# Attention projection by seven products: GpSimd's work given to VectorE, the rotation limited to 1024 tokens, block sums made in the out projection

## The reference

```python
hs = rms_norm(xs, norm_g[i]) * (1.0 + sc_s) + sh_s          # 1024 latent tokens; hp the same for 128 context tokens
q, k, v, g = jnp.split(h @ w_in, 4, axis=-1)                # w_in is 1024 x 8192, 8 heads of 256 in each of q, k, v, g
qs, ks_ = apply_rope(qs, cos, sin), apply_rope(ks_, cos, sin)   # x * cos + rot * sin, latent tokens only
out = gated_out(rms_norm(attend(q, k, v)) * c, g, w_out)    # (o * silu(g)) @ w_out
x = x + gate * out
```

## Time and profile before

| | |
|---|---|
| median of three runs | 2240.91 us |
| the profiled execution's own time | 2238.06 us |
| its span on the core | 2236.2 us |
| TensorE busy | 2135.9 us (96%) |
| VectorE busy | 1356.4 us (61%) |
| ScalarE busy | 888.6 us (40%) |
| GpSimd busy | 105.1 us (5%) |
| mean granted clock of TensorE | 0.985 |

### The profile page before, as it was taken

The page is one execution under the profiler, slowest core; times in us unless marked ns, Lnnn a source line. Parts: engine busy times, 40 slices in busy tenths (PEclk is TensorE's granted clock), DMA queues, the critical chain, the costliest instruction groups (busy, mean ns, idle before and its releaser), DMA issues. The chain is left out here.

```text
span 2236.2 us, 33058 instructions
## 1 busy us (share of the span) xinstructions
PE 2135.9 (96%) x13347; PEld 2035.8 (91%) x13347; DVE 1356.4 (61%) x2034; ACT 888.6 (40%) x1648; POOL 105.1 (5%) x44
## 2 busy tenths in 40 slices
PE   8999999989997999999999999999999999999997
PEld 3999877989997999999999999999999999989997
DVE  4777464763257877878755332228888888875223
ACT  4511142232123333333334243336666666665110
POOL 0000000000003222222200000000000000000000
PEclk9999999999998999999999999999999999999999
DMA  8455342784233444455545534443444433307332
GB/s 331 137 175 181 122 151 100 256 311 146 81 120 119 133 138 149 134 139 148 157 144 184 207 135 161 164 159 142 161 160 160 160 137 114 124 1 264 114 127 85
DMA packets 124824, 342.70 MB, mean 153 GB/s; under 512 B 14337, under 2 KB 69761, under 8 KB 114433
## 3 DMA queue, kind: packets, MB, share of 16 engines
q1 hardware_dynamic: 124672, 340.61, 44.5%
HBM read 225.70 MB, written 114.82 MB: 152 GB/s over the span
## 5 line engine op out<-in xcount | busy, mean ns | idle before, releaser
L2032 PE MATMUL o_ps<-o_y_hi,o_w 128*128 128x384 f32 x1536 | 395.0, 337 | 14.8 <-DVE o_y_lo L2141 13.3
L2032 PEld LDWEIGHTS o_ps<-o_y_hi,o_w 128*128 128x128 f32 x1536 | 280.3, 190 | 16.3 <-DVE o_y_lo L2141 13.7
L2032 PE MATMUL o_ps<-o_y_lo,o_w 128*128 128x384 f32 x768 | 258.4, 336 | 0.0
L2433 ACT ACTIVATE a_e<-a_ps,a_nmax 128x1152 f32<-128x1152 f32 x127 | 155.3, 1223 | 62.8 <-DVE a_nmax L2494 62.8
L2390 PE MATMUL a_ps<-a_v_hi,a_at_hi 128*128 128x256 f32 x576 | 173.0, 300 | 0.0
L2494 DVE TENSOR_REDUCE a_nmax<-a_ps 128x1 f32<-128x1152 f32 x127 | 171.8, 1353 | 0.2 <-PE a_ps L2357 0.2
L2390 PE MATMUL a_ps<-a_v_lo,a_at_hi 128*128 128x256 f32 x576 | 162.4, 282 | 0.0
L2390 PE MATMUL a_ps<-a_v_hi,a_at_lo 128*128 128x256 f32 x576 | 162.2, 282 | 0.0
L2032 PEld LDWEIGHTS o_ps<-o_y_lo,o_w 128*128 128x128 f32 x768 | 145.7, 190 | 0.0
L915 PE MATMUL p_ps<-p_late_hi,p_w_hi 128*128 128x384 f32 x384 | 128.9, 336 | 2.4 <-DVE p_late_lo L1202 2.3
L2141 DVE TENSOR_TENSOR o_y_lo<-o_y_raw,o_y_hi 128x384 fp32r<-128x384 f32 x96 | 51.9, 555 | 128.6 <-ACT o_y_hi L2086 128.4
(11 more groups left out here) (321 smaller groups left out, 5435.3 us busy)
## 6 DMA issues: line engine op xcount, KB each, us to landing
p_w_raw<-w_in_dram SPq DMA_DIRECT2D x32, 1024.0 KB, 6.9
o_y_raw<-y_dram SPq DMA_DIRECT2D x96, 192.0 KB, 3.6
g_wada<-w_ada_dram SPq DMA_DIRECT2D x16, 1024.0 KB, 6.8
f_w_raw<-w_u_dram SPq DMA_DIRECT2D x32, 512.0 KB, 4.3
o_w_raw<-w_out_dram SPq DMA_DIRECT2D x32, 512.0 KB, 4.3
g_dram<-g_stage SPq DMA_DIRECT2D x16, 576.0 KB, 3.2
f_g<-g_dram SPq DMA_DIRECT2D x8, 1152.0 KB, 7.6
y_dram<-f_y SPq DMA_DIRECT2D x8, 1152.0 KB, 5.3
```

Source lines behind the costliest of these rows:

```text
L2032: mm = pe.matmul(ps[:, d, 0:CH], a, m, start=(e == 0 and j == 0), stop=(e == ET - 1 and j == 2))
L2433: act.activation(split3(e[:, m % 2, half, :]), ps[:, 3 * half:3 * half + 3, 0:CH], ACT.Exp, bias=nmax[:, m % 2, half:half + 1], scale=1.0, ...
```

## The change

- GpSimd has no instruction left in `project`.
- The four input block sums are made by VectorE at the end of the out projection of layer 0 (`mix`, at tile 5), in place in the normed x (`block`) instead of in tiles of their own. To make room, the norm of the first 768 tokens moves from tile 4 to tile 2 and its high and low halves from tile 5 to tile 4.
- In `project`, VectorE makes the weight block sums of unit 1 and cuts t2 before it norms the late tokens; ACT cuts t2 and t0 before it copies the norm's factors. The order of the further cuts is new, and the eviction of unit 0 (`unload`) waits until the sums in whose place it writes are cut.
- The rotation's two additions are VectorE's, directly behind "third", and cover the 1024 latent tokens alone, as does the sine product. turned_lo(0) and turned_lo(1) move to before "far_near" and "near_far", ahead of the weight block sums. The block sums are in the order 0, 1, 2, 3, and the first pair's high half waits for two of them.
- In `values`, the weights for the next head are cut ahead of the fifth step (at == 4) and not ahead of the first.

```diff
+    def block(self, k, c):
+
+        return self.x[:, 4 * k:4 * k + 4, c * CH:(c + 1) * CH]
...
-        t_sum = [at(f"t{k}_sum", [P, DT // 2, CH], 24576 + 6144 * k) for k in range(4)]
+        t_sum = [tiles.block(k, c) for k, c in ((0, 0), (1, 1), (0, 1), (1, 0))]
...
                 if n == 1:
-                    pe.wait_ge(t_lo_done, 1)
+                    pe.wait_ge(t_lo_done, 3)
                 else:
                     pe.wait_ge(combined, summed(n - 1, "second"))
                 product(Z2, sums_of(1), mixed(1), True, True).then_inc(proj_done, 1)
                 pe.wait_ge(snapped, 2 * (n - 1) + 1)
                 product(Z1, weights(0, 1), quarter(1, 0), False, True).then_inc(proj_done, 1)
                 pe.wait_ge(s_lo_done, s_ready(n, 1))
-                if n == 1:
-                    pe.wait_ge(t_lo_done, 2)
-                else:
+                if n > 1:
                     pe.wait_ge(combined, summed(n - 1, "far_near"))
                 product(Z4, sums_of(2), mixed(2), True, True).then_inc(proj_done, 1)
-                if n == 1:
-                    pe.wait_ge(t_lo_done, 3)
-                else:
+                if n > 1:
                     pe.wait_ge(combined, summed(n - 1, "near_far"))
                 product(Z3, sums_of(0), mixed(0), True, True).then_inc(proj_done, 1)
...
-            for b in range(2):
+            act.wait_ge(t_summed, 4)
+            inverse_rms.root(act)
+            mixed_hi(2)
+            mixed_hi(0)
+            inverse_rms.copies(act)
+            for d in range(DT):
+                act.wait_ge(t_done, 2 * DT + d + 1)
+                for tok, which in PIECES:
+                    op = act.activation(tiles.late_hi[:, d, tok], tiles.x_late[:, d, tok], ACT.Identity,
+                                        bias=sh.mod[:, LAYER, d, which:which + 1])
+                op.then_inc(h_hi_done, 1)
+
+            def unload(b):
                 act.wait_ge(proj_done, made(0, f"late{b}"))
+                act.wait_ge(t_lo_done, 2)
                 act.copy(made_x[0][:, b, 0:2 * CH].rearrange("p (c t) -> p c t", c=2),
                          ps[:, WHOLE[b][0]:WHOLE[b][1] + 1:WHOLE[b][1] - WHOLE[b][0], 0:CH]).then_inc(evicted, 1)
                 act.copy(made_x[0][:, b, chunk(2)], ps[:, LATE[b], 0:CH]).then_inc(evicted, 1)
+
+            sums_hi(1, 0)
+            mixed_hi(1)
+            sums_hi(1, 1)
+            act.wait_ge(proj_done, made(0, "late0"))
+            tiles.split_hi(act, 1, 0)
+            unload(0)
+            mixed_hi(3)
+            unload(1)
...
-                if n >= 2:
+                if n == 1:
+                    act.wait_ge(t_lo_done, 4)
...
-                    turned_hi(n - 1, 0)
-                    if n + 1 < UNITS:
-                        sums_hi(n + 1, 0)
-                    turned_hi(n - 1, 1)
-                else:
-                    if n - ROPE in (2, 4):
-                        past_split((n - ROPE) // 2 - 1)
-                    if n + 1 < UNITS:
-                        sums_hi(n + 1, 0)
+                    for b in range(2):
+                        turned_hi(n - 1, b)
+                elif n - ROPE in (2, 4):
+                    past_split((n - ROPE) // 2 - 1)
+                if n + 1 < UNITS:
+                    sums_hi(n + 1, 0)
...
-                if j + 1 < H:
+                def next_hi():
...
                 for at, t in enumerate(ORDER):
+                    if at == 4 and j + 1 < H:
+                        next_hi()
...
+            def sums(n):
+
+                dve.wait_ge(raw_in[n % 2], 16 * (n // 2) + 16)
+                if n > 1:
+                    dve.wait_ge(proj_done, made(n - 1, "near_far"))
+                    dve.wait_ge(s_lo_done, s_ready(n - 1, 1))
+                dve.tensor_tensor(s_sum[:, 0], block_of(n, 1, 0), block_of(n, 1, 1), ALU.add).then_inc(s_summed, 1)
+                dve.wait_ge(s_summed, 4 * (n - 1) + 1)
+                dve.tensor_tensor(s_sum[:, 1], s_sum[:, 0], block_of(n, 0, 0), ALU.subtract).then_inc(s_summed, 1)
+                dve.tensor_tensor(s_sum[:, 2], block_of(n, 0, 0), block_of(n, 1, 0), ALU.subtract).then_inc(s_summed, 1)
+                dve.wait_ge(s_summed, 4 * (n - 1) + 2)
+                dve.tensor_tensor(s_sum[:, 3], block_of(n, 0, 1), s_sum[:, 1], ALU.subtract).then_inc(s_summed, 1)
...
-                    dve.wait_ge(t_summed, 4)
+                    dve.wait_ge(t_lo_done, 4)
...
-                dve.scalar_tensor_tensor(turned[:], made_x[n % 2][:], SCALE if n < H else 1.0,
-                                         cs[:, 1:2, :].to_broadcast([P, 2, T]), ALU.mult, ALU.mult).then_inc(sined, 1)
+                dve.scalar_tensor_tensor(turned[:, :, 0:NS], made_x[n % 2][:, :, 0:NS], SCALE if n < H else 1.0,
+                                         cs[:, 1:2, 0:NS].to_broadcast([P, 2, NS]), ALU.mult, ALU.mult).then_inc(sined, 1)
...
+            def rotate(n):
+                dve.wait_ge(cosined, n + 1)
+                for b in range(2):
+                    x = made_x[n % 2][:, b, 0:NS]
+                    dve.tensor_tensor(x, x, turned[:, 1 - b, 0:NS], ALU.add if b else ALU.subtract).then_inc(rotated, 1)
...
-            sums(1, (2, 0, 1, 3))
-            for k, m in enumerate((1, 2)):
-                mixed_lo(m, k + 1)
+            sums(1)
+            dve.wait_ge(shift_done, 1)
+            mixed_lo(2, 1)
+            for d in range(DT + 1):
+                if d < DT:
+                    norm(d)
+                if d > 0:
+                    low_half(d - 1)
+            mixed_lo(0, 2)
             sums_lo(1, 0)
-            mixed_lo(0, 3)
+            mixed_lo(1, 3)
+            tiles.split_lo(dve, 1, 0, w_ready(1, 0))
             sums_lo(1, 1)
             mixed_lo(3, 4)
-            tiles.split_lo(dve, 1, 0, w_ready(1, 0))
...
+                if n <= ROPE:
+                    rotate(n - 1)
                 dve.wait_ge(combined, summed(n, "third"))
                 dve.wait_ge(snapped, 2 * (n - 1) + 2)
                 dve.tensor_tensor(far(n)[:, chunk(1)], far(n)[:, chunk(1)], far(n)[:, chunk(0)], ALU.add).then_inc(combined, 1)
+                if n <= ROPE:
+                    turned_lo(n - 1, 0)
                 dve.wait_ge(combined, summed(n, "far_far"))
                 add(n, "far_near", far(n)[:, chunk(0)], Z4, near(n)[:, chunk(1)], "far_near")
-                dve.wait_ge(combined, summed(n, "far_near"))
-                add(n, "near_far", near(n)[:, chunk(1)], Z3, near(n)[:, chunk(1)], "near_far")
-                if n + 1 < UNITS:
-                    sums(n + 1, (2, 0, 1, 3))
-                if n <= ROPE:
-                    turned_lo(n - 1, 0)
-                if n + 1 < UNITS:
-                    sums_lo(n + 1, 0)
                 if n <= ROPE:
                     turned_lo(n - 1, 1)
                 elif n - ROPE in (2, 4):
                     past_split((n - ROPE) // 2 - 1)
+                dve.wait_ge(combined, summed(n, "far_near"))
+                add(n, "near_far", near(n)[:, chunk(1)], Z3, near(n)[:, chunk(1)], "near_far")
+                if n + 1 < UNITS:
+                    sums(n + 1)
+                    sums_lo(n + 1, 0)
...
-                if j + 1 < H:
+                def next_lo():
...
                 for at, t in enumerate(ORDER):
+                    if at == 4 and j + 1 < H:
+                        next_lo()
...
-        @block.gpsimd
-        def _(pool):
-            for semaphore in x_stored:
-                pool.wait_ge(semaphore, 16 * NCH)
-            pool.wait_ge(t_done, 2 * DT)
-
-            def x_of(k, c):
-                return tiles.x[:, 4 * k:4 * k + 4, c * CH:(c + 1) * CH]
-
-            pool.tensor_tensor(t_sum[0][:], x_of(0, 1), x_of(0, 0), ALU.subtract).then_inc(t_summed, 1)
-            pool.wait_ge(t_summed, 1)
-            pool.tensor_tensor(t_sum[1][:], x_of(1, 1), t_sum[0][:], ALU.subtract).then_inc(t_summed, 1)
-            pool.wait_ge(t_summed, 2)
-            pool.tensor_tensor(t_sum[2][:], x_of(1, 1), x_of(0, 1), ALU.subtract).then_inc(t_summed, 1)
-            pool.tensor_tensor(t_sum[3][:], x_of(1, 0), t_sum[1][:], ALU.subtract).then_inc(t_summed, 1)
-
-            def rotate(n, b):
-                pool.wait_ge(cosined, n + 1)
-                x = made_x[n % 2][:, b, :]
-                pool.tensor_tensor(x, x, turned[:, 1 - b, :], ALU.add if b else ALU.subtract).then_inc(rotated, 1)
-
-            for n in range(ROPE):
-                for b in range(2):
-                    rotate(n, b)
...
-                if following is not None and d == 5:
+                if following is not None and d == 4:
...
+            def mix(block):
+
+                near, far = [block(k, 0) for k in range(2)], [block(k, 1) for k in range(2)]
+                dve.wait_ge(following.h_lo_done, LAST * DT)
+                dve.tensor_tensor(near[0], far[0], near[0], ALU.subtract).then_inc(following.t_summed, 1)
+                dve.wait_ge(following.t_summed, 1)
```

(14 more changed lines are left out.)

52 lines of the change are left out of this document (10 added, 42 removed).

## The result

The changed kernel took 2187.79 us (median of 4 runs, 2185.70 to 2189.32), beside 2241.93 of the kernel before on the same chip (4 runs): a ratio of 0.9756 with an interval of 0.9738 to 0.9774. 2190.5 had been predicted, range 2184 to 2202. The medians differ by 54.1 where 50.4 was forecast; of the 3.7 between, 1.0 went to the kernel before, which took 2241.93 here and not 2240.91. The profiled execution took 2189.32, its span is 2187.5.

The account below looks back on a forecast made before the run. TensorE was taken as busy nearly everywhere, so only its idle or low-clock stretches could give time: 10.3 + 2.8 + 26.9 + 10.4 = 50.4 us off 2238.06, plus 2.85 to the median, gives 2190.5, range 2184 to 2202.

Parts of the forecast that it names:

- The start of the stage and unit 1: Project stage: late norm without GpSimd's sums beside it, 11.2 us less up to unit 1; unit 1 itself 2.8 less.
- rival 4: The clock falls in the 1.6 us gap before unit 1 and the tail costs 3.5: 2196 us, 3 in 100.
- The tail: End of the out projection: norm moved earlier and block sums added on VectorE delay tile 7's eviction, 0.9 us lost.
- The value stage: Head 0: weight conversion behind the fourth eviction removes TensorE's wait and the lower clock behind it, 10.4 us saved.
- Rival 2: The value stage keeps its wait, the gate's store landing over 2.7 us later: 2200 us, 6 in 100.
- Units 2 to 16: Rotation units of the attention projection: pitch falls from 24.79 to 23.0 us, 26.9 us saved over 15 units.
- The ring: Rotation units: sine waits for the previous unit's low-half stores, cut after block sums, setting the pitch (24.0 and 25.7 us).
- Rivals 1 and 5: Low-half stores still late (2198 or 2205 us, 12 in 100); ring lengthens (2249, 1 in 100) or VectorE bounds (2231, 1).

Follow-up runs that it names:

- Experiment 5: Kernel before, with GpSimd's four input block sums made by VectorE at the project stage's start, ahead of the late norm: 2232.84 us against 2239.46 (0.9974).
- experiment 4: Kernel before, with only the value stage's move, the next head's weights cut behind the fourth eviction: 2230.46 us (0.9951).
- Experiment 1: Kernel before, with VectorE's low halves and ScalarE's high halves moved ahead of the weight block sums, GpSimd still rotating: 2217.16 us (0.9894).
- experiment 9: Kernel before, with ScalarE's new order alone, both high halves ahead of its weight-sum cast: 2217.34 us (0.9906).
- Experiment 3: Changed kernel with VectorE's old order of low halves and weight block sums, rotation staying on VectorE: 2189.67 us (0.9771).
- experiment 10: Changed kernel with both old orders, VectorE's low halves and ScalarE's second high half, rotation staying on VectorE: 2199.57 us (0.9825).
- experiments 2: Changed kernel with the rotation's two additions back on GpSimd, 1024 tokens: 2188.01 us (0.9763).
- Experiments 6 to 8: Changed kernel with one, two and three extra 1.22 us VectorE products per rotation unit, ahead of cosine: 2187.91, 2202.01 and 2241.69 us.

## Why the prediction was right

- **The start of the stage and unit 1** came out at 11.3 and 2.8, as worked out. Experiment 5 gives 7.15 of the first its cause, the sums on GpSimd beside the late norm. The other 4.2 come with the new order of the cuts ahead of unit 1, which no run took alone. The 1.36 of idle time was predicted as 1.6, on ScalarE's eviction, and the clock did not fall behind it: unit 1 took 22.96. So rival 4 did not come.
- **The tail** lost 0.6 in place of 0.9, by the way that was worked out. The trace after runs 2.26 us later from tile 2 on (its last matmul at 629.63 and not at 627.37). With that taken off, the norms start at 635.05 and 640.34 (predicted 635 and 640), the block sums at 658.5 (658.5), and tile 7 is evicted at 670.1 (670.4); tile 3 was late, for which nobody waited. In the eight traces that have this code the loss is 0.3 to 0.7.
- **The value stage** gave 10.4 as predicted, and 10.8 alone in experiment 4. Rival 2 did not come: ScalarE asked for the gate's store right behind the fourth eviction and had it 0.37 us later, 13.2 us into the stage (13.4 before), and the fifth eviction ended at 1249.52, 3.6 us before TensorE's eighth step (1253.12) wanted its bank.
- **Units 2 to 16** gave 28.7 where I had 26.9: the pitch is 22.88, not 23.0. I had read 22.9 from the unit itself and took 23.0 from the gate units. Those had a wait of their own, 0.2 every second unit, which has also gone (the 1.0 of units 17 to 23). These two are all of the difference between 50.4 and 53.6, but for 0.4 in the tail and at the start. The gate units' wait came of VectorE's cut of the cached keys and values (`past_split`), which stood right ahead of the weight split in units 18 and 20. In the kernel before, VectorE ahead of unit 21, which starts at 1202.27:

```profile
1198.79 2.28 DVE L1268 TENSOR_TENSOR p_past_lo<-p_past_raw,p_past_hi 128x2048 fp32r<-128x2048 f32 x1
1200.99 1.22 DVE L200 TENSOR_TENSOR p_w_lo<-p_w_raw,p_w_hi 128x1024 fp32r<-128x1024 f32 x1
```

  The split ends at 1202.21 and holds TensorE. Experiment 1 moved this cut forward with the low halves and has 22.88 in units 18 to 21; experiment 9 left it and has 23.02 and 23.22 by turns. Experiment 3 has it late again and still 22.88: there the weight block sums, in their new order, are done earlier, and the split ends 0.4 us ahead of the unit.
- **The ring** was rightly named, and its stores' landing was its largest part, but I gave the gain to VectorE's order and the rotation. That step's account fell. The prediction said that "only after the block sums does DVE cut the second low half", and took the 6.3 to 8.05 of landing as what a store costs. The runs show that the late cut is no harm when the high stores leave early (experiment 3: 22.93; experiment 9: 23.23). An early cut alone was not run and can't be: it needs the second high half, which in ScalarE's old order stands behind sums that VectorE would make only after the cut. The landing measured from a late cut is 4.1 to 4.6 when the high stores have gone, and 7.3 when they are issued right ahead. Before, the second high half stood on ScalarE behind the weight sums, though GpSimd had it ready at 778.25; in the trace of before ScalarE made it at 781.28. The forecast of the units held all the same, since it was worked out with every edit in place: in the changed kernel the high stores are again right ahead of the early low ones, and in the key units the low halves land at T+24.0 to T+25.1 (predicted 24.9), 0.6 to 1.7 us before sine wants them. Only the account of which edit gives the gain was wrong, and experiment 3's forecast of 2200 to 2215 missed for it.

  Units 2 to 16 in us, by what each kernel has of the change:

| kernel | ScalarE's order | VectorE's order | rotation | units 2 to 16 |
|---|---|---|---|---|
| before | old | old | GpSimd, 1152 tokens | 371.9 |
| experiment 9 | new | old | GpSimd, 1152 | 348.5 |
| experiment 1 | new | new | GpSimd, 1152 | 347.4 |
| experiment 10 | old | old | VectorE, 1024 | 355.1 |
| experiment 3 | new | old | VectorE, 1024 | 344.0 |
| experiment 2 | new | new | GpSimd, 1024 | 343.2 |
| changed | new | new | VectorE, 1024 | 343.2 |

  The gains do not add: ScalarE's order gives 23.4 with the old rotation and 11.1 with the new one, and the new rotation gives 16.8 with both old orders (experiments 2, 3 and 10 have the new order of the weight block sums as well, which counts with it). The last 4.2, from experiment 1 to 2, come of the 1024 tokens or of the new order of the weight block sums; no run separates these.
- **Rivals 1 and 5** did not come: sine waits for no store, though VectorE is as busy as before. Experiments 6 to 8 put the reserve ahead of "third" at about 1.7 us of work per unit; beyond it every us costs one, and behind waits of 2 us the clock took 1.5 more in 9 of 15 units.

## What to carry to other kernels

When an engine waits for a store, ask what stands ahead of that store in its in-order queue, and which engine made that late. Here one cast moved on ScalarE took the store's landing from 6.3 to 8 us to about 4 and gave 23 us by itself, more than the new rotation, which the rewrite seems to be about (16.8 with the block sums' new order, and nothing for the engine once the order is right). Before you give an engine more work, count its reserve on the chain to the next engine's wait, and not its share of busy time: VectorE at 84 per cent took another 1.2 us per unit for nothing, and at two more it set the pitch while it was still idle 2.1 us per unit. A second cause can be hidden behind the first, so undo the parts one at a time and also two together: experiment 3 alone would have acquitted the order altogether.
